# In the up stage, the rounding of each weight unit's high part moves from GpSimd to ScalarE

## The reference

```python
h = rms_norm(x, norm_ffn_g[l])
up = causal_dwconv(h @ w_up[l], conv_ffn_w[l])      # w_up: 1024 x 5632, 3 taps in time
a, b = jnp.split(up, 2, axis=-1)
x = x + (jax.nn.silu(a) * b) @ w_down[l]
```

## Time and profile before

| | us |
|---|---|
| median of 3 runs | 2464.92 (2463.43 to 2466.97) |
| profiled execution, its time | 2463.95 |
| profiled execution, its span from first to last instruction | 2462.2 |
| PE busy over the span | 2320.3 |
| up stage, first to last matmul | about 415 to 657 |
| from its last matmul to the first of the down stage | about 657 to 665 |

### The profile page before, as it was taken

How to read it: one execution, slowest core, us unless ns; L and a number is a source line. 1 busy time by engine, 2 the same in 40 slices (tenths; PEclk the granted TensorE clock), 3 DMA queues, 4 the chain that set the end, 5 groups by cost and what they waited for, 6 DMA issues and landing times.

```text
span 2462.2 us, 53138 instructions
## 1 busy us (share of the span) xinstructions
PE 2320.3 (94%) x22099; PEld 1802.7 (73%) x22099; DVE 1237.0 (50%) x2255; ACT 965.1 (39%) x1837; POOL 1161.5 (47%) x785
## 2 busy tenths in 40 slices
PE   8899997999899499999999999999799899999898
PEld 6778885888786357777766677677689787777776
DVE  3453252999701715555555555555440375655521
ACT  3112212555401345555555555555421344334300
POOL 4445564777566433433344443333436444433345
PEclk9999998999999799999999999999899999999999
DMA  3223232333231121222222222222413322212212
GB/s 109 75 76 79 77 95 60 94 96 100 78 102 52 62 63 55 64 72 64 64 65 72 72 72 81 66 64 63 169 51 110 104 76 58 59 41 56 82 60 94
DMA packets 261806, 187.85 MB, mean 76 GB/s; under 512 B 17227, under 2 KB 241353, under 8 KB 261081
## 3 DMA queue, kind: packets, MB, share of 16 engines
q1 hardware_dynamic: 261593, 184.76, 25.2%
HBM read 162.69 MB, written 22.04 MB: 75 GB/s over the span
## 4 chain that ended last, share of the span: by engine, by line
PE 59%; DVE 2%; POOL 1%; DMA 1%; issue 1%; ACT 1%; SPq 0%; POOLq 0%; DVEq 0%
PE ps L1247 18%; PE ps L158 7%; PE ps L159 6%; PE ps L160 6%; PE ps L1405 3%; PE ps L1421 3%; PE ps L1447 2%; PE ps L2235 2%; PE ps L1394 1%; PE ps L1361 1%; PE ps L1333 1%; PE ps L1256 1%; PE ps L220 1%; PE ps L2221 1%; DMA z_lo<-z_kept 1%
## 5 line engine op out<-in xcount | busy, mean ns | idle before, releaser
L146 POOL TENSOR_SCALAR w_hi<-raw 128x1024 fp32r<-128x1024 f32 (+1 forms) x196 | 223.3, 1139 | 602.7 <-PE ps L160 584.6
L149 POOL TENSOR_TENSOR w_lo<-raw,w_hi 128x1024 fp32r<-128x1024 f32 (+1 forms) x196 | 490.8, 2504 | 16.3
L158 PE MATMUL ps<-h_hi,w_hi 128*128 128x512 f32 x648 | 257.8, 398 | 16.3 <-ACTq L889 16.3
L159 PE MATMUL ps<-h_lo,w_hi 128*128 128x512 f32 x648 | 254.4, 393 | 0.0
L160 PE MATMUL ps<-h_hi,w_lo 128*128 128x512 f32 x648 | 254.2, 392 | 0.0
L1247 PE MATMUL ps<-mixed_r,raw 128*64 128x264 f32 x1024 | 156.4, 396 | 23.9 <-DVE omka L2585 20.5
L1739 POOL TENSOR_TENSOR kp<-k_b,kp 128x528 f32<-128x528 f32 x16 | 21.0, 1315 | 328.0 <-ACT kp L1542 328.0
L158 PEld LDWEIGHTS ps<-h_hi,w_hi 128*128 128x128 f32 x648 | 123.5, 191 | 42.0 <-issue 17.1
L160 PEld LDWEIGHTS ps<-h_hi,w_lo 128*128 128x128 f32 x648 | 122.9, 190 | 26.2
L159 PEld LDWEIGHTS ps<-h_lo,w_hi 128*128 128x128 f32 x648 | 123.2, 190 | 25.0
L1247 PE MATMUL ps<-mixed_k,raw 128*64 128x264 f32 x1024 | 138.3, 389 | 0.0
(11 more groups left out here) (410 smaller groups left out, 5993.3 us busy)
## 6 DMA issues: line engine op xcount, KB each, us to landing
raw<-in_rwkv_w_in_dram SPq DMA_DIRECT2D x64, 512.0 KB, 4.1
raw<-in_w_up_dram SPq DMA_DIRECT2D x44, 512.0 KB, 3.8
raw<-in_w_in_dram SPq DMA_DIRECT2D x41, 512.0 KB, 3.9
raw<-in_w_down_dram SPq DMA_DIRECT2D x22, 512.0 KB, 3.3
raw<-in_mla_w_in_dram SPq DMA_DIRECT2D x22, 512.0 KB, 4.0
sb_kept<-xT SPq DMA_DIRECT2D x16, 528.0 KB, 2.7
xT<-sb_kept SPq DMA_DIRECT2D x16, 528.0 KB, 4.5
raw<-in_rwkv_w_out_dram SPq DMA_DIRECT2D x16, 512.0 KB, 4.2
```

Source lines behind the costliest of these rows:

```text
L146: nc.gpsimd.tensor_scalar(w_hi[s][:, 0:width], raw[s][:, 0:width], 1.0, 0.0, ALU.mult, ALU.add).then_inc(split_hi, 1)
L149: nc.gpsimd.tensor_tensor(w_lo[s][:, 0:width], raw[s][:, 0:width], w_hi[s][:, 0:width].bitcast(F32), ALU.subtract).then_inc(split_ready, 1)
L158: nc.tensor.matmul(dst, w[0], x[0], start=start, stop=False)
L159: nc.tensor.matmul(dst, w[0], x[1], start=False, stop=False)
```

## The change

In the up stage's loop, GpSimd no longer calls `split_unit`. ScalarE rounds the high part of the unit two ahead, between the eviction (L894) and the first tap (L896) of the unit that PE has just finished, after a wait for the landing of the unit's DMA. GpSimd waits for `split_hi` and makes only the low part.

```diff
             def _(pool):
                 with pool.Fori(1, KF + 1) as i:
                     for ab in range(2):
-                        split_unit(pool, 2 * i + (U_UP + ab), (U_UP + ab) % 2)
+                        s = (U_UP + ab) % 2
+                        pool.wait_ge(split_hi, 2 * i + (U_UP + ab + 1))
+                        nc.gpsimd.tensor_tensor(w_lo[s][:, 0:1024], raw[s][:, 0:1024], w_hi[s][:, 0:1024].bitcast(F32),
+                                                ALU.subtract).then_inc(split_ready, 1)
+                        pool.wait_ge(split_ready, 2 * i + (U_UP + ab + 1))
...
                         nc.scalar.activation(up_raw[:, ab, 2:2 + T1], ps[:, (U_UP + ab) % 2, :], ACT.Copy).then_inc(up_out, 1)
+                        s = (U_UP + ab) % 2
+                        act.wait_ge(landed[s], 16 * i + landings(U_UP + 2 + ab, s))
+                        nc.scalar.activation(w_hi[s][:, 0:1024], raw[s][:, 0:1024], ACT.Copy).then_inc(split_hi, 1)
                         act.wait_ge(up_out, 2 * i + (ab + 2))
                         nc.scalar.activation(up_c[:, ab, 0, :], up_raw[:, ab, 2:2 + T1], ACT.Copy,
```

## The result

| | before | after |
|---|---|---|
| median, us | 2465.31 (6 runs, 2463.43 to 2466.97) | 2474.80 (6 runs, 2473.85 to 2476.11) |
| ratio after/before | | 1.0039, 95% interval 1.0026 to 1.0052 |
| profiled execution's span, us | 2462.2 | 2473.1 |

The kernel is slower by 9.5 us, where 9.8 was forecast; its time is 2474.80 us, forecast 2474.7. The forecast was counted from 2464.92, the median of the first 3 runs of the kernel before.

The account below looks back on a forecast made before the run. PE was taken to bound the up stage; 21 waits of 0.45 us (9.5) plus 0.3 us at the stage's end made 9.8 us, which on 2464.92 gave 2474.7 us. The range was 2469.0 to 2483.0.

Parts of the forecast that it names:

- the deadline is E+5.28: Up stage: E is the end of a unit's last matmul; weights split from then must be ready 5.28 us later.
- The chain of a: Iteration's first unit: table load, eviction, rounding, subtraction end 5.57 us after its last matmul; 0.45 us late, 21 times.
- restart: PE after waiting for a low part: second matmul follows 0.34 us later instead of 0.23, costing 0.11 more.
- The sign that was named: Up stage, profile after: PE's matmul at L158 waits for POOL's L149 some 21 times for 0.2 to 0.4 us.
- Units b have no wait: Iteration's second unit, without table load: low part 5.03 us after its last matmul at most, before the 5.28 deadline.
- DVE is out of the way: Up stage: DVE finishes 1 us before POOL's next subtraction for unit a, and is never late for ACT.
- the mean of L912: Profile sign, up stage: the mean time of this source line falls after the change.
- The last chain: End of the up stage, DVE's chain into the down stage: POOL ends later, 0.3 us more.
- Hidden after all: Rival, up stage: low part comes in time, only the tail's 0.3 us shows, 2465.3 us; chance 0.10.
- Turns with DVE: Rival, up stage: POOL's subtraction for a waits up to 0.6 us more for DVE, 12.6 in all, 2487; chance 0.07.
- further load: Rival on ACT: another table load, 1.28 us per iteration, 27 us, or slower rounding; 2500 and more; chance 0.02.
- The drain of 1.38 us: Skill page's rule for each ACT table switch, beside the 1.28 load; would add 29 us; forecast left it out.

Follow-up runs that it names:

- e1: Changed kernel, but ScalarE rounds the high part of units b only and GpSimd splits units a whole; 2465.1 us against 2465.02 for the kernel before, ratio 1.0002.
- e3: Changed kernel with ScalarE's rounding put ahead of the wait for the taps and the eviction; 2464.96 us against 2465.02 for the kernel before, ratio 1.0001.
- e8: Changed kernel with a 4-column copy as first ScalarE instruction of each iteration, ahead of the wait; 2465.1 us against 2464.82 for the kernel before, ratio 0.9999.
- e2: Changed kernel, but ScalarE rounds the high part of units a only and GpSimd splits units b whole; 2474.85 us against 2465.02 for the kernel before, ratio 1.0044.
- e4: Changed kernel with a 4-column ScalarE copy added behind silu; 2474.89 us against 2465.02 for the kernel before, ratio 1.0044.
- e5: Changed kernel with a second, unused 1024-column ScalarE copy ahead of the rounding of units a only; 2493.52 us against 2465.63 for the kernel before, ratio 1.0116.
- e6: Changed kernel with a second, unused 1024-column ScalarE copy ahead of the rounding of units b only; 2475.09 us, ratio 1.0039 to the kernel before.
- e7: Kernel before, without the moved rounding, with up and down stages in one block; 2454.38 us against 2465.63 for the kernel before, ratio 0.9954.
- e9: Changed kernel with the small copy at the iteration's head and both stages in one block; 2455.18 us against 2464.82 for the kernel before, ratio 0.9958.

## Why the prediction was right, point by point

*PE is the bound, and the deadline is E+5.28.* Right. Kernels whose chain ends ahead of it (e1, e3, e8) have the time of the kernel before; those whose chain ends behind it (after, e2, e4, e5, e6) do not.

*The chain of a.* Step by step, forecast and measured, in us from E:

| | forecast | after |
|---|---|---|
| table load | 0.11 to 1.39 | 0.11 to 1.39 |
| eviction | 1.40 to 2.00 | 1.40 to 2.00 |
| rounding | 1.97 to 3.03 | 1.90 to 2.95 |
| subtraction | 3.17 to 5.57 | 3.02 to 5.42 |
| PE's next unit | 5.62 | 5.48 |
| lengthening of the iteration | 0.45 | 0.37 |

The term that was off is the overlap of eviction and rounding: 0.10 (537.66 + 0.60 to 538.16), near the upper of the two values that the rows gave (0.11), not 0.03; another 0.07 came from POOL's start, 0.07 behind ACT's end (539.21 to 539.28) where the row that was taken had 0.14. Part of this was given back at the restart. The unit is 0.20 late, not 0.34, but the iteration is longer by 0.37, not 0.31: after the 0.34 to the second matmul, the next few are 0.23 to 0.24 us apart instead of 0.227, which makes 0.17 for a restart where the forecast had 0.11 from two rows. In all, 7.9 us in the stage against 9.5 forecast. The sign that was named, waits of 0.2 to 0.4 us, holds for how late the unit is (0.20); the waits that the view lists at the weight load are longer, 0.46 on average.

*Units b have no wait.* Right (e1_only_b, and e6_double_b, which has 0.95 more in its chain: POOL ends at E+5.09 there).

*DVE is out of the way.* Right: L876 takes 2.40 for a. One sign was wrong: the mean of L912 (now L919) did not fall. It is 1.51 us, 1.40 before. POOL's subtraction now starts 0.7 us ahead of the first of VectorE's two taps, which ends only after it and takes up to 2.28 us instead of 0.75. What fell is L922 (now L929), from 2.69 to 0.69, and L920 (now L927), from 1.05 to 0.43.

*The last chain*: 0.08 us more instead of 0.3.

*The sum*, 9.8 forecast and 9.5 measured, is closer than its terms, and that is luck: 8.0 us are shown in the stage and its last chain, and about 1.5 of the median's difference are not. In the profiled executions they lie in stages that were not edited. One such place can be read. Behind the gap at the meeting of the engines, the down stage starts with matmuls 0.43 us apart instead of 0.227, and there the granted clock is 0.50, the 1.2 GHz level (1.00 and 0.99 right behind it). This lasts for 3.7 us before and for 6.0 us after, which costs 1.1 us more (windows view of both, columns as in rows 2):

```profile
664.70:668.40 3.70, 3.69 (x9) 2.96 (x10) 0.00 (x0) 0.00 (x0) 0.00 (x0) 0.50 0.53 164
673.50:679.50 6.00, 5.98 (x14) 4.74 (x15) 0.00 (x0) 0.00 (x0) 0.00 (x0) 0.50 0.57 187
```

The nine kernels with the two blocks line up by how long this lasts. The time from the first matmul of the down stage to the first L203 is 122.36 to 122.43 us in those with 8 steps of over 0.4 us (before, e1, e5, e8), 122.62 with 9 (e3), 122.79 with 10 (e2), 123.10 with 11 (e6), 123.53 with 13 (e4) and 123.58 with 14 (after). The part of the medians' differences that the stage and its last chain don't show has much the same order: -0.7 us in e5, 0.2 in e2, 0.4 in e6, 1.9 in e4, 1.5 in the changed kernel. And the granted clock of whole executions is 0.971 to 0.974 in the changed kernel and 0.971 to 0.973 in e4, but 0.973 to 0.975 before and 0.974 in e5. So much of the 1.5 us is likely time at the lower clock, though each trace is of one execution. Why the low stretch is longer in one kernel and not in another is open: both ends occur among kernels with waits (e5_double_a 122.42, e4_load_early 123.53), and no run tells whether the change has a part in it. The forecast had no term for it.

*The rivals.* "Hidden after all" falls for the changed kernel, and holds for it once the table load (e8) or the eviction (e3) is out of the chain; that was the point from which it decides. "Turns with DVE" did not occur in the changed kernel for units a. No further load was added. The load ahead of a copy, which the rival "hidden after all" set against the trace, is what e4_load_early and e8_load_at_head explain: it went with the place in the loop, not with the copy. The drain of 1.38 us was not there: the eviction starts 0.01 after the load, and the load 0.02 after an ACT instruction where nothing else is waited for (532.27 in e8_load_at_head, behind silu's end at 532.25). The time agrees with the rows, not with the rule of the Trainium skill (ScalarE: Activation LUTs, "What ACT_TABLE_LOAD costs") that the prediction set beside them.

## What to carry to other kernels

Moving an instruction to an idler engine moves it into that engine's order: what counts is the chain from the event that frees its buffer to its deadline on the bounding engine, with everything that the new engine does ahead of it, table loads included. Busy shares said the opposite of what happened here: POOL and DVE together lost 115 us of work in the stage's window, and PE waited. When a chain has to take on such an instruction, put it first in the chain (e3) or let ScalarE's table load happen in idle time (e8); either was enough here, and gave back the time of the kernel before, no more. And look first for the places where PE has no work at all: one block for two stages gained 11.3 us (e7), more than the changed split cost.

## What the runs showed of the hardware that was not expected

- In the up stage's loop a load of ScalarE's table stands at the first ScalarE instruction of the body in every iteration (22 x 1.28 us), behind that instruction's wait, though a copy behind silu runs without one (e4_load_early). An instruction of 0.2 us at the head of the body, ahead of the wait, moves the load (e8_load_at_head).
- After a wait of a few tenths of a microsecond, PE's matmuls are slow beyond the first one: 0.34 and then 0.23 to 0.24 us apart against 0.227, at a granted clock of 1.00 in the window.
- A gap of 7.6 to 9.0 us ahead of the down stage was followed by 8 to 14 steps of 0.43 us from matmul to matmul (the first one 0.56), at a granted clock of 0.50 to 0.51, in nine kernels whose code in that place is the same. In the two kernels without the gap (e7, e9) the matmuls there are 0.23 us apart.
